# Hybrid decoder step on Trainium2: the loops of the projections and of the output exchanged, so that chunks or column halves alternate under each weight block

## The reference

```python
h = rms_norm(x, norm_pre)
proj = jnp.einsum('btd,dc->btc', h, w_in)
(a_u, a_g, b_q, b_k, b_v, b_i, b_f, b_o, b_g,
 c_q, c_k, c_v, c_g, d_q, d_g) = jnp.split(proj, SPLIT_POINTS, axis=-1)
...
mix = jnp.concatenate([ya, yb, yc, yd], axis=-1)
out = rms_norm(jnp.einsum('btc,cd->btd', mix, w_out), norm_post)
return x + out, st
```

## Time and profile before

| | |
|---|---|
| median of 3 runs | 1955.6 us (1943.92 to 1960.59) |
| profiled execution: span, its own time | 1957.4 us (from the first to the last instruction; no other time of it is given) |
| PE busy | 1538.7 us (79%), 7351 matmuls |
| PEld busy | 1103.1 us (56%), 7351 loads |
| DVE, ACT, POOL busy | 787.1, 534.1, 453.0 us |
| mean granted clock of PE | 0.863 of full speed |
| DMA | 236.97 MB, mean 121 GB/s |

### The profile page before, as it was taken

How to read it: one execution, slowest core, us unless ns; L and a number is a source line. 1 busy time by engine, 2 the same in 40 slices (tenths; PEclk the granted TensorE clock), 3 DMA queues, 4 the chain that set the end, 5 groups by cost and what they waited for, 6 DMA issues and landing times. The chain is left out here.

```text
span 1957.4 us, 25676 instructions
## 1 busy us (share of the span) xinstructions
PE 1538.7 (79%) x7351; PEld 1103.1 (56%) x7351; DVE 787.1 (40%) x1289; ACT 534.1 (27%) x991; POOL 453.0 (23%) x335
## 2 busy tenths in 40 slices
PE   3114434679999998999994889898969999958997
PEld 3001210266356347338323889898958988935786
DVE  5264454035435536535531243232334544533221
ACT  5000000014523523532531232324222322222120
POOL 0365464054255346237220000000000000000000
PEclk7556666778998998999896899999979989979999
DMA  4568786453355255245220331212033132144321
GB/s 129 191 202 281 237 268 233 134 161 125 95 169 161 75 169 168 76 147 170 87 95 14 98 106 35 88 44 75 23 92 101 43 106 71 32 164 137 98 86 54
DMA packets 201962, 236.97 MB, mean 121 GB/s; under 512 B 13410, under 2 KB 124352, under 8 KB 201896
## 3 DMA queue, kind: packets, MB, share of 16 engines
q1 hardware_dynamic: 177776, 190.91, 31.6%
q10 hardware_dynamic: 20608, 34.61, 5.4%
q0 software_dynamic: 3520, 10.82, 1.5%
HBM read 215.88 MB, written 20.64 MB: 121 GB/s over the span
## 5 line engine op out<-in xcount | busy, mean ns | idle before, releaser
L242 PE MATMUL bank<-xh,b_w_hi 128*128 128x344 f32 x480 | 160.4, 334 | 29.6 <-DVE b_w_lo L227 29.6
L1666 POOL TENSOR_TENSOR p_keys<-p_keys,p_q 128x1024 f32<-128x1024 f32 x64 | 149.3, 2351 | 112.2 <-DMA p_keys<-cache_sb_k 111.9
L1666 POOL TENSOR_TENSOR cp_keys<-cp_keys,cp_q 128x1024 f32<-128x1024 f32 x64 | 158.7, 2498 | 66.9 <-DMA cp_keys<-cache_sb_k 52.1
L242 PE MATMUL bank<-xl,b_w_hi 128*128 128x344 f32 x480 | 156.7, 326 | 0.0
L242 PE MATMUL bank<-xh,b_w_lo 128*128 128x344 f32 x480 | 156.6, 326 | 0.0
L494 POOL TENSOR_TENSOR c_later<-c_later,c_L 128x512 f32<-128x512 f32 (+3 forms) x96 | 96.4, 1005 | 243.3 <-PE bank L547 226.7
L242 PE MATMUL bank<-xh,d_w_hi 128*128 128x344 f32 x384 | 129.3, 337 | 24.3 <-DVE d_w_lo L227 24.3
L242 PE MATMUL bank<-xh,c_w_hi 128*128 128x344 f32 x384 | 125.8, 328 | 21.1 <-DVE c_w_lo L227 18.3
L1734 PE MATMUL bank<-p_values,p_page_A 128*8 128x512 f32 x256 | 70.8, 833 | 77.8 <-DMA p_values<-cache_sb_v 43.7
L242 PE MATMUL bank<-xl,d_w_hi 128*128 128x344 f32 x384 | 125.6, 327 | 0.0
L242 PE MATMUL bank<-xh,d_w_lo 128*128 128x344 f32 x384 | 125.5, 327 | 0.0
(11 more groups left out here) (386 smaller groups left out, 2949.7 us busy)
## 6 DMA issues: line engine op xcount, KB each, us to landing
p_values<-cache_sb_v ACTq DMA_DIRECT2D x128, 256.0 KB, 3.9
p_keys<-cache_sb_k SPq DMA_DIRECT2D x128, 256.0 KB
cp_keys<-cache_sb_k SPq DMA_DIRECT2D x128, 256.0 KB, 2.8
cp_values<-cache_sb_v SPq DMA_DIRECT2D x128, 256.0 KB, 2.7
b_w_raw<-w_in SPq DMA_DIRECT2D x20, 512.0 KB
c_w_raw<-w_in SPq DMA_DIRECT2D x16, 512.0 KB
d_w_raw<-w_in SPq DMA_DIRECT2D x16, 512.0 KB
o_mix<-mix SPq DMA_DIRECT2D x8, 1024.0 KB, 6.0
```

The costliest lines, as they stand in the source:

```text
L242: last = self.nc.tensor.matmul(self.banks[c][:, 0:self.width], w[:, s, k, :], x[:, k, c * self.width:(c + 1) * self.width], start=(k == 0 ...
L1666: self.nc.gpsimd.tensor_tensor(self.keys[:, s], self.keys[:, s], q, ALU.mult).then_inc(self.scaled.sem, 1)
```

## The change

In `multiply` the loop over the three chunks becomes the innermost: each weight tile is used for the three chunks in turn, into banks 0, 1 and 2, before the next product begins. The waits for `taken` stand ahead of the first three matmuls of a block, one each, and the last three matmuls of a block raise `projected`, one each. `before_last` is called ahead of the sixth of the eight weight tiles, so behind 45 matmuls of 72; before, it stood behind 48. In `products` the loop over the two halves becomes the inner one. The number of matmuls, their operands and shapes, the DMAs and the work of all other engines stay. (After the change the lines behind `multiply` are one higher.)

```diff
--- before.py
+++ after.py
@@ -232,17 +232,18 @@
         s = j % self.slots
         pe.wait_ge(self.hi_ready.sem, self.hi_ready.at(i, j + 1))
         pe.wait_ge(self.lo_ready.sem, self.lo_ready.at(i, j + 1))
-        for c in range(self.chunks):
-            if c == self.chunks - 1 and before_last:
+        for k in range(KT):
+            if k == 5 and before_last:
                 before_last()
-
-            pe.wait_ge(self.taken.sem, self.taken.at(i, self.chunks * (j - 1) + c + 1))
-            for k in range(KT):
-                for n, (w, x) in enumerate(((self.hi, self.xh), (self.hi, self.xl), (self.lo, self.xh))):
-                    last = self.nc.tensor.matmul(self.banks[c][:, 0:self.width], w[:, s, k, :],
-                                                 x[:, k, c * self.width:(c + 1) * self.width],
-                                                 start=(k == 0 and n == 0), stop=(k == KT - 1 and n == 2))
-            last.then_inc(self.projected.sem, 1)
+            for n, (w, x) in enumerate(((self.hi, self.xh), (self.hi, self.xl), (self.lo, self.xh))):
+                for c in range(self.chunks):
+                    if k == 0 and n == 0:
+                        pe.wait_ge(self.taken.sem, self.taken.at(i, self.chunks * (j - 1) + c + 1))
+                    one = self.nc.tensor.matmul(self.banks[c][:, 0:self.width], w[:, s, k, :],
+                                                x[:, k, c * self.width:(c + 1) * self.width],
+                                                start=(k == 0 and n == 0), stop=(k == KT - 1 and n == 2))
+                    if k == KT - 1 and n == 2:
+                        one.then_inc(self.projected.sem, 1)
 
     def take(self, act, i, j, out, func, scale=1.0):
 
@@ -2076,8 +2077,8 @@
 
             def products(b, kk):
 
-                for h in range(2):
-                    for n, (m, w) in enumerate(((hi, w_hi), (hi, w_lo), (lo, w_hi))):
+                for n, (m, w) in enumerate(((hi, w_hi), (hi, w_lo), (lo, w_hi))):
+                    for h in range(2):
                         last = nc.tensor.matmul(ACC[b][h][:, :], m[:, b, kk, :], w[:, kk, h * H:(h + 1) * H],
                                                 start=(kk == 0 and n == 0), stop=(kk == KO - 1 and n == 2))
                 return last
```

## The result

The changed kernel takes **1970.6 us** (median; 1965.4 to 1974.7) against 1955.6: the ratio is 1.008, with a 95% interval of 1.005 to 1.011, so between 10 and 22 us slower. The prediction said 1956 with a range of 1930 to 1975: the time lies in the range, but only because the range was drawn to take in rival 2 (1972, no gain from banks). It is that rival's time, and not that of the forecast.

A forecast was written before the change was run, and what follows sets the result against it. The tensor engine was taken as the bound. Later takes cost 14.3 us, bank changes gave back 14.1, net +0.2 us on a 1957.4 us span whose runs have median 1955.6: forecast 1956 us, range 1930 to 1975.

The forecast's parts named there:

- rival 2: Projections and output: changing banks gains nothing, so the 14.3 us of waits stand alone, 1972 us; chance 0.17.
- Part (c): Projections: all three chunks end together, ScalarE's last take comes 0.39 us later; waits cost 14.3 us in all.
- c_ 0 to 1 (direct): Stick-breaking, block following block directly: the first three matmuls each wait for a take, 0.93 us per boundary.
- b_ block 4, next pass: mLSTM block 4: three more matmuls behind ScalarE's squares, 0.47 us, partly hidden by ScalarE, leaving 0.2 us.
- the 0.39 behind block 3 of the stick-breaking stage: Block 3's takes stand in DVE's and ACT's queues ahead of the softmax: 0.39 us in each of four passes.
- The restarts: From a take's end to the waiting matmul's start: 0.10 us assumed, bounds 0.06 and 0.33.
- Step (b): Projections and output: neighbouring matmuls in different PSUM banks run closer together, saving 10.8 and 3.3 us, 14.1 in sum.
- The 6.5 ns: Output, 512 columns: saving per change of bank, mean 0.2228 us over 239 distances; 512 distances give 3.3 us.
- The 3.1 ns: Projections: saving per change of bank, 102 distances averaging 154.3 ns against 157.4 for 3452 others; 10.8 us in all.
- both ends, 0 and 53 us: Projections' bank gain: 0 if tied to a single bank change, 53 us if all 14 ns vanish from 3816 matmuls.
- Part (a): Neighbouring matmuls with one stationary operand: each still brings its own weight load, so reuse is worth 0.
- the prediction's rivals: Those meant: rotation frees the pipeline, 1908 us, 0.13 with kept weights; pauses lower the clock, 1982 us, 0.10 with other clock losses.

The follow-up runs named there:

- first by: Changed kernel, but the first of eight weight tiles goes chunk by chunk and the other seven rotate; 1967.8 us, ratio 1.0071.
- last by: Changed kernel, but the last of eight weight tiles goes chunk by chunk and the first seven rotate; 1958.4 us, ratio 1.0027.
- middle rotating: Changed kernel, but the first and last weight tiles go chunk by chunk and only the six between rotate; 1956.7 us, ratio 1.0007.
- takes held: Kernel before, no loop exchanged; its three chunks are announced to ScalarE together behind the block's last matmul; 1972.1 us, ratio 1.0083.
- the projections alone: Kernel before with only the loops of `multiply` exchanged, `products` as before; 1969.6 us, ratio 1.0079.
- the output alone: Kernel before with only the loops of `products` exchanged, halves inside; 1954.0 us, ratio 1.0009.
- half loads: Kernel before, but weight tiles 1, 3 and 5 load and multiply only 64 of 128 stationary columns; 1956.6 us in one run.

## Why the prediction was wrong by 15 us

**Part (c) was right wherever its terms could be measured.** The distance from E to the seventh matmul of the next block, past all waits, in us, median over the passes, from the trace's nanoseconds; the columns are the increase over before. Block 4 counts its own length too, the gates' term runs to the next stage's first matmul:

```
                        before  predicted  after  first by  last by  middle   takes
                                                  chunks    chunks   rotates  held
c_ 0 to 1 (direct)       1.11     0.93     0.88    0.49      0.51    -0.01    0.82
c_ 1 to 2                1.96     0.05     0.03    0.01      0.02     0.02    0.00
b_ 0 to 1 (direct)       1.11     0.93     0.88    0.49      0.50    -0.01    0.81
b_ 1 to 2                4.73     0.39     0.38    0.38      0.00     0.00    0.70
b_ block 4, next pass             0.20     0.20    0.20      0.00     0.00    0.04
d_ 0 to 1                5.63     0.39     0.39    0.39      0.02     0.00    0.71
d_ 2 to 3                4.33     0.20     0.13    0.13      0.00     0.00    0.45
g_ to the next stage              0.39     0.41    0.38     -0.02     0.06    0.67
```

In the changed kernel they repeat from pass to pass within 0.03; that of block 4 is read in the three passes that another follows. The column "after" gives 2.89 x 4 + 0.41 = 12.0 us. Not found is the 0.39 behind block 3 of the stick-breaking stage: the 32nd matmul behind E moves by 0.4 to 3.5 us between the four passes of one and the same kernel. Its mean over the passes is E+19.0 before, 18.7 after and 19.1 with the takes held, so no trace shows those 1.6 us. The slower stream adds 0.5 ns x 69 x 53 = 1.8. Sum 13.8, or 15.4 with the term not found, beside 10 to 22 measured. The other columns, with the slower stream in the share of the tiles that rotates, give 10, 6, 1 and 15 us; measured are 14 (9 to 19), 5 (1 to 10), 1 (-2 to 5) and 16 (10 to 22). The restarts, put at 0.10 behind a take, are nearer to the lower bound: the first take begins at E+0.04 and lasts 0.46, and the matmul starts at E+0.55, 0.05 behind its end.

The two profiled executions differ by only 6.4 us (1957.4 and 1963.8). The execution after was already 1.7 us ahead at the first block of the stick-breaking stage, where nothing is exchanged yet, and had 2 us less of half clock in its projections and output (187 matmuls against 194, of which 6 against 23 the long ones). One execution isn't a measure for 15 us; the distances against E are.

**What the prediction did not have: the clock in the mLSTM stage.** By stage the execution after is 1.7 us shorter ahead of the stick-breaking stage, 2.6 longer in it, 0.6 longer in the gates, 8.9 in the mLSTM stage, 1.2 shorter in the memory stage and 2.8 in the output. The mLSTM stage has grown by more than its terms, (0.88 + 0.38 + 0.20) x 4 = 5.8. Its first three passes, from block 0 to block 0, last 86.9, 85.9 and 85.7 us before, and 88.4, 88.2 and 88.5 after: 1.5, 2.3 and 2.8 more, where the terms give 1.46. At the end of a pass PE waits for weights (5.01 us before, 4.75 after), and the next pass begins at half clock. The first 6 us of the second and third pass, PE only, before and then after:

```profile
1170.10:1176.10 6.00, 5.95 (x27) 0.69 0.77 217
1256.00:1262.00 6.00, 5.91 (x29) 0.73 0.81 220
```

```profile
1173.10:1179.10 6.00, 5.91 (x22) 0.54 0.78 220
1261.40:1267.40 6.00, 5.97 (x21) 0.50 0.78 214
```

A clock of 0.69 and 0.73 over 6 us means 3.7 and 3.2 us at half clock, 0.54 and 0.50 mean 5.5 and 6.0. Half of the growth is lost: 0.9 and 1.4 us, which is what these two passes have grown beyond their terms. The same two stretches read 0.53 and 0.50 with the projections alone and 0.56 and 0.51 with the takes held, but 0.67 and 0.72 with the output alone and 0.72 and 0.72 with the middle rotating. So in these traces the later takes go together with some 2 us of half clock in this stage. That they cause it isn't shown, with one profiled execution of each kernel; in the memory stage the half clock costs between 12 and 21 us (an estimate: half of PE's busy time at half clock) in the eleven traces, without such an order.

**Step (b) failed: "A change of bank saves 6.5 ns at 512 columns" and "I take 3.1 ns there".** Neither gain came: with a new bank each time the distances are 227.1 instead of 227.2 ns, and 157.8 instead of 157.3. So the 14.1 us that were to cancel the waits are missing. The two figures had two different faults.

- *The 6.5 ns were rounding.* They came from timeline rows, which give starts to 10 ns. In a steady stream three matmuls mostly take 680 ns, a whole number of such steps, and the rounding falls on the same place each time: 0.23, 0.23, 0.22, again and again (the third reads 0.22 in 179 of 239 cases). With the trace's nanoseconds the same three distances are 227.3, 226.7 and 227.5 ns. Averaging 239 rows doesn't help where the error repeats; and the three averages of the prediction sum to the same 681.5 ns, which could have been a warning, as the gain of one distance was the loss of two others.
- *The 3.1 ns belonged to two places in the program, not to the bank.* Each of the 71 distances in a block has its own mean, and it repeats over the 53 blocks. Before the change, with the number of the distance (0 to 70), only 23 and 47 lead to a new bank:

```
distance          14     19     23*    32     34     38     47*    68
before, ns      161.0  152.6  152.9  161.6  152.5  152.4  155.8  163.5
after, ns       156.0  156.4  155.9  158.4  159.9  162.0  157.2  155.4   (all lead to a new bank)
```

Distances as short as that of 23 stand at 19, 34 and 38, where the bank stays, and after the change the short ones are elsewhere (24 with 152.2, 60 with 152.4). The 102 samples of the prediction were two places, seen 53 and 49 times. The comparison with "the 3452 others" needed the spread over places, from 152 to 163, and not the many repeats. After the change the places spread from 152 to 169. What makes the pattern isn't settled; in the kernel with half loads it is partly another.

The prediction had both ends, 0 and 53 us, and took "the nearest rows". With the gain at its lower end the sum was rival 2's, 1972. That the measured time still fell into the range shows that the range was wide enough, not that the sum was right.

**Part (a) was right:** no reuse of the stationary operand, loads as many as matmuls. **Two rules of the prediction's rivals.** The granted clock is 1.00 in the eight stretches behind the new pauses. The Trainium skill (TensorE: Matmul & The Clock Gate, "A second HAM failure mode: psum-queue depth-cycling") tells of a kernel that went through PSUM banks with short idles between, and whose clock swung. These eight stretches don't show that. With rotating banks a matmul of 344 columns takes 157.8 ns in the stream. The Trainium skill (same page, "Back-to-back issue gap") gives N/2.4 + 2.5 ns for a lone gap when warm, an estimate of 145.8 ns for 344 columns. The traces don't reach it, before or after.

## What to carry to other kernels

When a loop exchange makes several accumulations end together, count who takes them out of PSUM and in which queue: three takes that stand 0.35 us apart cost 0.88 us wherever the next block needs the banks at once, and 0.39 wherever something waits for the last of them. Rotating in the middle, with the chunks started and finished one by one, costs nothing that could be measured (-2 to +5 us), so the end and the start of the loop decide, not its body. And before a few ns per instruction are multiplied by thousands, ask how many different places in the program they were read at, and whether the view's rounding can make them.

## What the runs showed of the hardware

- At full clock each matmul of a stream costs its columns at 2.4 GHz and some 14 ns: 157.3 - 143.3 = 14.0 at 344 columns, 227.2 - 213.3 = 13.9 at 512. At half clock it costs only its columns at 1.2 GHz: 287 ns (344 / 1.2 = 286.7) and 427 ns (512 / 1.2 = 426.7). Within 1 ns the 14 ns depend neither on whether the bank changes, nor on whether the stationary operand does, nor on how many of its columns are loaded (64 or 128), nor on the number of moving columns (344 or 512). What they are stays open.
- Within a block the distances differ by their place, 152 to 163 ns before the change and 152 to 169 after, and repeat over 53 blocks.
- From the end of a take to the waiting matmul's start it is 0.05 us, and the matmul behind that start comes 0.26 us later (0.35 where it waits for the next take).
